# A four-sublayer decoder trunk: two more projections in 512-column form, five state-space tables and twenty modulation rows in other places

## The reference, cut to what matters

```python
cs = silu(c)
for i in range(2):
    mod = cs @ ada_w[i] + ada_b[i]                  # 2048 -> 6 * 2048
    sh1, sc1, g1, sh2, sc2, g2 = split(mod, 6)
    h = rms_norm(x, norm1_g[i]) * (1 + sc1) + sh1
    mix = dilated_attention(h, w_in, w_out) if i == 0 else s5_mixer(h, ...)
    x = x + g1 * mix
    h = rms_norm(x, norm2_g[i]) * (1 + sc2) + sh2
    x = x + g2 * conv_ffn(h, w_up[i], conv_w[i], conv_b[i], w_down[i])   # F = 5632
return rms_norm(x, final_norm_g)
```

## Time and profile before

| what | value |
|---|---|
| time, median of 3 runs | 2733.81 us (2732.66 to 2735.42) |
| time of the profiled execution | 2732.6 us |
| its span (first to last instruction) | 2730.6 us |
| PE busy | 2658.2 us, 97% of the span |
| DVE busy | 2303.9 us, 84% |
| ACT / POOL busy | 1291.1 / 519.4 us |
| HBM traffic | 266 GB/s over the span |

### The profile page before, as it was taken

How to read it: one execution, slowest core, us unless ns; L and a number is a source line. 1 busy time by engine, 2 the same in 40 slices (tenths; PEclk the granted TensorE clock), 3 DMA queues, 4 the chain that set the end, 5 groups by cost and what they waited for, 6 DMA issues and landing times.

```text
span 2730.6 us, 50020 instructions
## 1 busy us (share of the span) xinstructions
PE 2658.2 (97%) x18412; PEld 2375.5 (87%) x18412; DVE 2303.9 (84%) x3390; ACT 1291.1 (47%) x1852; POOL 519.4 (19%) x466
## 2 busy tenths in 40 slices
PE   5999999999999999999999999999999999999998
PEld 2998888888898888888889999999788888888887
DVE  7978988888889999899999989998898975677755
ACT  2444444444434555435555344444365553455542
POOL 4242211101132111000111322244311110011122
PEclk8999999999999999999999999999999999999999
DMA  9989988889876887678888967779777766656663
GB/s 388 385 269 339 347 312 333 318 313 336 312 228 234 297 281 250 204 247 312 280 283 270 376 221 239 235 254 330 258 253 241 257 184 188 196 187 189 182 189 109
DMA packets 241978, 725.45 MB, mean 266 GB/s; under 512 B 51074, under 2 KB 60034, under 8 KB 240898
## 3 DMA queue, kind: packets, MB, share of 16 engines
q1 hardware_dynamic: 185184, 666.98, 71.1%
q10 hardware_dynamic: 56612, 56.01, 6.4%
HBM read 701.66 MB, written 25.44 MB: 266 GB/s over the span
## 4 chain that ended last, share of the span: by engine, by line
PE 83%; DVE 5%; POOL 1%; issue 1%; DMA 1%; ACT 1%; ACTq 0%; POOLq 0%; DVEq 0%
PE proj L1910 39%; PE proj L1913 22%; PE proj L1933 5%; PE proj L1934 4%; PE proj L1935 4%; PE proj L1915 3%; PE proj L1928 1%; DVE w_lo L1181 1%; PE proj L1931 1%; PE ps L2049 1%; PE ps L2139 1%; ACT w_hi L600 1%; DVE ada L1071 0%; DVE work L1115 0%; DVE work L1463 0%
## 5 line engine op out<-in xcount | busy, mean ns | idle before, releaser
L600 ACT ACTIVATE w_hi<-raw 128x1024 fp32r<-128x1024 f32 (+1 forms) x896 | 934.6, 1046 | 999.4 <-PE proj L1913 362.2
L1181 DVE TENSOR_TENSOR w_lo<-raw,w_hi 128x1024 fp32r<-128x1024 f32 (+1 forms) x896 | 1104.8, 1236 | 285.9 <-ACT w_hi L600 275.7
L1910 PE MATMUL proj<-h_hl,w_hi 128*128 128x512 f32 x3990 | 1007.5, 393 | 2.7 <-DVE x L1510 1.8
L1910 PEld LDWEIGHTS proj<-h_hl,w_hi 128*128 128x128 f32 x3990 | 730.5, 189 | 139.3 <-DVE x L1510 2.1
L1913 PEld LDWEIGHTS proj<-h_hl,w_lo 128*128 128x128 f32 x4256 | 580.6, 190 | 41.6
L1913 PE MATMUL proj<-h_hl,w_lo 128*128 128x256 f32 x4256 | 593.4, 282 | 0.0
L1071 DVE SCALAR_TENSOR_TENSOR ada<-ada,held 128x1024 f32<-128x1024 f32 x304 | 396.0, 1303 | 0.0
L1813 POOL TENSOR_TENSOR a_hl<-work,a_hl 128x256 fp32r<-128x256 f32 (+1 forms) x88 | 120.6, 1371 | 1137.3 <-ACT a_hl L880 1137.3
L1933 PE MATMUL proj<-a_hl,w_hi 128*128 128x256 f32 x864 | 245.6, 284 | 0.7 <-DVE a_hl L1401 0.6
L1934 PE MATMUL proj<-a_hl,w_hi 128*128 128x256 f32 x864 | 244.5, 283 | 0.0
L1935 PE MATMUL proj<-a_hl,w_lo 128*128 128x256 f32 x864 | 244.5, 283 | 0.0
(11 more groups left out here) (273 smaller groups left out, 2870.3 us busy)
## 6 DMA issues: line engine op xcount, KB each, us to landing
raw<-in_w_up SPq DMA_DIRECT2D x352, 512.0 KB, 4.9
ada<-in_ada_t SPq DMA_DIRECT2D x304, 512.0 KB, 5.7
raw<-in_w_in SPq DMA_DIRECT2D x224, 512.0 KB, 6.5
raw<-in_w_down SPq DMA_DIRECT2D x128, 448.0 KB, 3.5
raw<-in_w_down SPq DMA_DIRECT2D x64, 512.0 KB, 3.6
ada<-in_ada_w SPq DMA_DIRECT2D x48, 512.0 KB, 8.6
raw<-in_w_out SPq DMA_DIRECT2D x32, 512.0 KB, 5.1
raw<-in_ssm_w_in SPq DMA_DIRECT2D x32, 512.0 KB, 4.9
```

Source lines behind the costliest of these rows:

```text
L600: nc.scalar.activation(w_hi[:, j % LAG, 0:nk * P], raw[:, j % s.ring, 0:nk * P], ACT.Copy).then_inc(hi_ready, 1)
L1181: V.tensor_tensor(w_lo[:, j % LAG, 0:nk * P], raw[:, j % s.ring, 0:nk * P], w_hi[:, j % LAG, 0:nk * P].bitcast(F32), ALU.subtract).then_in ...
L1910: ins = mm(both, w_hi[:, j % LAG, w], hl[:, k].rearrange("p c t -> p (c t)"), start=(k == 0), stop=False)
```

## The change

`attn_out` and `down0b` become wide stages. The 16 tables are no longer all made in `attn_out`: eleven are (steps 3, 5, 7, 10, 12, 15, 17, 20, 22, 25 and 27), and five in `down0b` (steps 16, 21, 26, 31 and 36), in other places of `work` and in `acc`. The 16 modulation rows of `down0b` and four of the eight of `up0b_end` move into `qkv`: its iterations 1 to 5 now have 28 rows in 28 steps. The take of part 19 moves from `down0b` to `up0b_end`. Waits for the last tables' stores move behind `down0b`.

```diff
-WIDE = {"qkv", "up0a", "up0a_end", "down0a", "up0b", "up0b_end", "ssm_out", ...
+TABLES_FIRST = 11
+WIDE = {"qkv", "attn_out", "up0a", "up0a_end", "down0a", "up0b", "up0b_end", "down0b", "ssm_out", ...
@@
-    add("qkv", 6, 14, two, ..., rows=spread(24, 28), begin=spread(20, 20, 8))
+    add("qkv", 6, 14, two, ..., rows=spread(28, 28), begin=spread(20, 20, 8))
@@
-    add("up0b_end", 1, 8, two, rows=spread(8, 16))
-    add("down0b", 1, 16, down, rows=spread(16, 34, 6))
+    add("up0b_end", 1, 8, two, rows=spread(4, 16))
+    add("down0b", 1, 16, down)
@@
+        ef_late, o = cut(work, 2400, 2, 4, 8, 8)
+        tab_a_late, o = cut(work, o, 8, 8, 8)
+        tab_b_late, o = cut(work, o, 8, 8, 8)
+        tab_o_late = [cut(work, o, 8, 64)[0], cut(acc[:, :], 0, 8, 64)[0]]
+        def table_step(n):
+            return 3 + 27 * n // TABLES_FIRST if n < TABLES_FIRST else 16 + 5 * (n - TABLES_FIRST)
@@ ACT
-                    for n in range(KT):
-                        late.setdefault(max(2 * n, 2), []).append(factors(n))
-                        late.setdefault(2 * n + 4 if n > 1 else 4, []).append(store_tab(n))
+                if name in ("attn_out", "down0b"):
+                    for n in range(TABLES_FIRST) if name == "attn_out" else range(TABLES_FIRST, KT):
+                        late.setdefault(max(table_step(n) - 3, 2), []).append(factors(n))
+                        late.setdefault(table_step(n) + 2, []).append(store_tab(n))
@@
-            TAKES = {"up0a_end": (14, 13, 3), "up0b_end": (14, 16, 3), "down0b": (45, 19, 1), ...
+            TAKES = {"up0a_end": (14, 13, 3), "up0b_end": (14, 16, 4), ...
@@ DVE
-                if name == "attn_out":
-                    for n in range(KT):
-                        late.setdefault(2 * n + 2 if n > 1 else 3, []).append(table(n))
+                if name in ("attn_out", "down0b"):
+                    for n in range(TABLES_FIRST) if name == "attn_out" else range(TABLES_FIRST, KT):
+                        late.setdefault(table_step(n), []).append(table(n))
```

More of the change, by code:

```diff
@@ L58 @@
 ADA = 4
-WIDE = {"qkv", "up0a", "up0a_end", "down0a", "up0b", "up0b_end", "ssm_out", "up1a", "up1a_end", "down1a", "up1b",
+TABLES_FIRST = 11
+WIDE = {"qkv", "attn_out", "up0a", "up0a_end", "down0a", "up0b", "up0b_end", "down0b", "ssm_out", "up1a", "up1a_end", "down1a", "up1b",
         "up1b_end", "down1b"}
@@ L139, in plan @@
     add("qkv1", 1, 28, [(PIECE, PIECE, True)], ring=7, old={10 + 2 * k: k for k in range(8)})
-    add("qkv", 6, 14, two, ring=7, old={j: 8 + j for j in range(8)}, rows=spread(24, 28), begin=spread(20, 20, 8))
+    add("qkv", 6, 14, two, ring=7, old={j: 8 + j for j in range(8)}, rows=spread(28, 28), begin=spread(20, 20, 8))
     add("attn_out", 1, 16, two)
@@ L775, in plain, with factors, f, store_tab @@
                 late = {}
+                def factors(n):
+                    def f(i):
+                        act.wait_ge(scores_done, HEADS)
+                        if n >= TABLES_FIRST:
+                            act.wait_ge(gated_ready, FB)
+                        wait(act, tab_made, n - 1)
+                        act.dma_start(table_place(n)[0].rearrange("p a b c -> p (a b c)"), ef_d[n]).then_inc(ef_in_s[n % 2], 16)
+                    return f
+                def store_tab(n):
+                    def f(i):
+                        act.wait_ge(tab_made, n + 1)
+                        act.dma_start(tab_d[n], table_place(n)[3].rearrange("p a b -> p (a b)")).then_inc(tab_out[n % 2], 16)
+                    return f
                 if name == "attn_out":
@@ L911, in _ @@
             for q in range(2):
-                act.wait_ge(tab_out[q], 16 * KT // 2)
+                act.wait_ge(tab_out[q], 16 * ((TABLES_FIRST + 1 - q) // 2))
             def load_tab(n):
@@ L932, in _ @@
                 act.wait_ge(bp_out[q], 16 * KT // 2)
+                act.wait_ge(tab_out[q], 16 * KT // 2)
             act.wait_ge(mod_ready, 20)
@@ L1206, in split_first @@
                 low(st[name])(0, LO_FIRST - 1)
-            TAKES = {"up0a_end": (14, 13, 3), "up0b_end": (14, 16, 3), "down0b": (45, 19, 1), "gate": (33, 20, 1),
+            TAKES = {"up0a_end": (14, 13, 3), "up0b_end": (14, 16, 4), "gate": (33, 20, 1),
                      "ssm_out": (33, 21, 1), "up1a": (41, 22, 1), "up1a_end": (47, 23, 1)}
@@ L1590, in _ @@
                                                                 4: [head1_low]}, keep=True))
-            dve.wait_ge(tab_out[0], 16 * KT // 2)
+            dve.wait_ge(tab_out[0], 16 * ((TABLES_FIRST + 1) // 2))
             norm(1, 0, 3 * KT, 10)
             split_first("ssm_in", ffn(0))
+            dve.wait_ge(tab_out[1], 16 * KT // 2)
             norm(2, 1, 0, 16)
@@ L1851, in _ @@
                 pool.wait_ge(bp_out[q], 16 * KT // 2)
+                pool.wait_ge(tab_out[q], 16 * KT // 2)
             G.memset(c_wide, 0.0).then_inc(cw_clear, 1)
```

25 lines of the change are left out of this document (10 added, 15 removed).

## The result

The changed kernel takes 2738.10 us (median of 20 runs, 2734.79 to 2740.39); the kernel before took 2733.07 in the 20 runs beside it (2731.00 to 2736.92). The ratio is 1.0015, with a 95% interval of 1.0009 to 1.0021: slower by 2.5 to 5.7 us. 2740.0 was forecast, 2735.5 to 2744 as the range.

The account below looks back on a forecast made before the run. PE was taken to set the pace, with DVE nearly full in down0b and attn_out. Terms +9.4 - 0.5 - 0.2 - 3.5 + 0.5 + 0.5 = +6.2 us gave 2738.8 profiled, 2740.0 as median; range 2735.5 to 2744.

Parts of the forecast that it names:

- qkv's heads: qkv loop: new rows at steps 13 and 27 delay POOL's mix, ten heads at 0.94 us each, +9.4 us.
- Rival 1: qkv: POOL's mix ends within its 0.97 us of room, the loop costs nothing, 2730.6 us; chance 0.07.
- Rival 2: qkv: a row locks out one POOL instruction for 1.2 us at most, 0.2 us a head, 2732.9 us; chance 0.06.
- mutual slowing: qkv, beside a head's mix: DVE and POOL slow each other, row 1.76 us instead of 1.2, POOL's last instruction 1.48 instead of 0.61.
- attn_out: attn_out: DVE's 5.67 us per block binds over PE's 5.59; net -0.5 us, and -0.2 at its end.
- the start: Start of attn_out: a table between splits 5 and 6 and two more instructions, mostly covered by PE's piece in hand, 0.8 us.
- down0b: down0b: PE's wide blocks gain 3.5 us, the last tables cost 0.5, the added instruction before the norm +0.5.
- The cushion's terms: down0b: 7.7 us of lead less w_hi 1.05, split 1.22, tail and add 0.9, hand-overs 0.3, written as 4.1 us.
- Rival 3: attn_out and down0b: DVE's backlogs stay within the cushions, PE gains in full, +3.4, 2737.2 us; chance 0.12.
- rival 4: attn_out and down0b: DVE becomes the bound in both, the wide form gives nothing, 2743.5 to 2745 us; chance 0.15.
- The rest: Elsewhere: four rows less in up0b_end, later waits for tab_out and the take of part 19 are free.
- The estimate that the prediction made by the Trainium skill: Wide k-tiles: 327 ns narrow against 325 wide, so 554 k-tiles gain 1.2 us; the rows' 5.9 was used instead.

Follow-up runs that it names:

- experiment 1: Changed kernel with no row at qkv steps 13 and 27 of iterations 1 to 5, two each at steps 3 and 17 instead: 2729.51 us.
- experiment 3: Changed kernel with the rows at qkv steps 13 and 27 of iterations 1 to 5 reading their second operand from PSUM, not SBUF: 2729.36 us.
- Experiment 4: Changed kernel with experiment 1's row places, ten tables in attn_out, later at its start, and six in down0b: 2729.76 us.
- experiment 5: Changed kernel with all modulation rows left where the kernel before has them, 16 of them in down0b: 2745.49 us.
- experiment 2: Kernel before with only the rows moved (20 into qkv, out of up0b_end and down0b), nothing made wide: 2742.68 us.
- Experiment 6: Changed kernel with all 16 tables in attn_out, so down0b is wide with neither rows nor tables: 2745.05 us.

## Why the prediction held, step by step

**qkv's heads, forecast +9.4, measured +8.7.** The step was right: the transposes wait for POOL ten times more, 0.66 us each where 0.7 was said, and the block takes 6.8 instead of 6.9. The head of the earlier trace rows was the right measure; the others have 0.06 us less idle. The second half of the step, that the queue, the bytes and the ten rows of steps 6 and 20 are free, is shown by experiment 1. Rival 1 fell to the ten waits. Rival 2 priced the exclusion at one instruction's length; its mechanism is the right one (experiment 3), its price was not, since POOL's chain holds two instructions there and each was stretched (1.60 and 1.48 against 0.74 and 0.61): 1.73 us, less PE's room of 0.97, is 0.76, against the 0.66 seen. What the prediction called a mutual slowing is this exclusion.

**attn_out, forecast -0.7 with its end, measured -0.4, and the reason given was wrong.** The prediction said that DVE's turn of 5.67 us would bind in every block, with DVE above 95%. It did not: from 813.55 on the block ends are 5.59 apart, PE's own pace, and over the stage DVE is busy for 90%. The step that failed is the price of a table. The prediction took 1.92 us, a table alone, out of a turn of 5.56 in which the table ran beside POOL's squares of x. In the kernel before (the table of 788.54 ends where the next split starts):

```profile
787.57 1.52 POOL L1693 TENSOR_TENSOR square<-x 128x256 f32<-128x256 f32 x1 [8.82 <-DVE x L1510]
789.17 1.07 POOL L1695 TENSOR_TENSOR sumsq<-sumsq,square 128x256 f32<-128x256 f32 x1
791.43 1.22 DVE L1181 TENSOR_TENSOR w_lo<-raw,w_hi 128x1024 fp32r<-128x1024 f32 x1
```

That table took 791.43 - 788.54 = 2.89 us, half as much again as the 1.92 of the one at 779.75, which has no POOL instruction beside it. With 2.89 the same sum gives 5.56 - 2.89 + 0.47 + 0.81 x 2.89 = 5.48 us, under PE's 5.59, and in the kernel after DVE duly has idle time again in the later blocks, first here:

```profile
837.48 1.77 DVE L1201 TENSOR_TENSOR w_lo<-raw,w_hi 128x1024 fp32r<-128x1024 f32 x1 [0.60 <-ACT w_hi L615]
```

What ate the gain was the start, put at 0.8 us: the four block times behind 789.07 are 6.14, 6.18, 6.08 and 6.08, 2.1 us above four of 5.59. There the tables of steps 5, 7, 10 and 12 leave DVE no gap, and a turn with a table in it is 5.56 + 0.47 = 6.03 us. Experiment 4 takes these waits away with the same forms and nearly as many tables, and the stage gains 2.0 us. That the term came out within 0.3 us is luck: a loss in every block was forecast, and one in four blocks was found.

The last head's 0.3 us (its wait is 0.89 here, 0.46 before) came on top and was put at nothing. There, too, POOL's mix lies beside tables and splits of DVE, and its six instructions take 5.45 us in the kernel before, 5.70 in the kernel after and 5.65 in experiment 5, stretched in different places. All experiments have 20.25 to 20.52 us there, experiment 5 with the rows as before and experiment 2 without the wide form among them, so no single edit is its cause; why is left open.

**down0b, forecast -2.5 with its end, measured -2.3.** The blocks come in 7.69 us up to 1579, and then three in 7.87, 8.01 and 7.84: 0.66 us for the last tables, where 0.5 was said. The norm's wait grew by 0.72 (1.13 to 1.85), where the tail's 0.47 was counted. Experiment 6, with no table here, has 124.86 and a wait of 1.65. That the backlog came out so near is in part luck, too: a table took 2.47 to 2.89 us here as well, where 1.92 was counted, and a block without one takes DVE 105.1 / 16 = 6.6 us in experiment 6, where 6.97 was counted, and the two errors offset each other. (The cushion's terms give 4.2, not the 4.1 written.) Rival 3, no stall in either stage, and rival 4, DVE as the bound in both, both fell: each stage stalled in a part of it only.

**The rest, forecast nothing, measured -0.7 in the profiled pair** (-1.6, +0.6, -0.8 and +1.0). These parts have the same work, but the first of them differs by kernel, as said below the table: some -1.7 us that the prediction left out. Of the terms, +8.7 + 0.3 - 0.4 - 2.3 = +6.4 us before rounding stands against the forecast's +6.2; the profiled pair has 5.7, the medians 5.0. So the sum was nearer to the truth than its parts, by an error in `qkv` of -0.7 against +0.3, +0.3 and +0.2 elsewhere.

The estimate that the prediction made by the Trainium skill (TensorE: Matmul & The Clock Gate, section Back-to-back issue gap) is 2.5 ns a k-tile before rounding, 1.4 us for 554 k-tiles and not 1.2. The rows were the better guide: PE's blocks of 16 k-tiles come 5.59 us apart in `attn_out` where 5.76 was the narrow pace, 10 ns a k-tile.

## What to carry to other kernels

An idle gap of an engine is free only if nothing else uses what the gap leaves open: before filling one, look at what runs on POOL in that very gap, and count each instruction of its chain once. When work must move, choose the place within the stage by that, since here two of 28 places held the whole cost of moving 20 rows. The price of an instruction is to be taken where it will run: a table cost DVE 1.92 us alone and 2.89 beside POOL, within one stage, and a sum that mixed the two named the wrong bound. Where a stage's mean load is near that of the bound, its start and end are to be counted apart from its middle.

## What the runs showed of the hardware

The granted clock behind a short idle time of PE is not the same from profile to profile. Ahead of the first matmuls of the stage after `down0a` PE waits 1.74 to 1.76 us in all nine kernels; the eight matmuls behind it then took 2.09 to 2.12 us in seven of them, and 2.73 and 3.21 in the kernel after and experiment 5. The three timelines (before, after, experiment 5):

```profile
1246.25 2.11 PE L1910 MATMUL proj<-h_hl,w_hi 128*128 128x512 f32 x8 [1.75 <-DVE x L1510]
```

```profile
1252.63 2.73 PE L1934 MATMUL proj<-h_hl,w_hi 128*128 128x512 f32 x8 [1.75 <-DVE x L1532]
```

```profile
1243.74 3.21 PE L1934 MATMUL proj<-h_hl,w_hi 128*128 128x512 f32 x8 [1.76 <-DVE x L1532]
```

The windows behind it, of before and of after (the clock is the third number from the end):

```profile
1246.00:1249.00 3.00, 2.75 (x15) 2.41 (x16) 2.83 (x13) 0.00 (x0) 0.00 (x0) 1.00 0.74 254
```

```profile
1252.50:1255.00 2.50, 2.37 (x8) 1.96 (x9) 2.36 (x12) 0.00 (x0) 0.00 (x0) 0.78 0.88 290
1255.00:1258.00 3.00, 3.00 (x14) 2.68 (x14) 2.96 (x8) 1.33 (x2) 0.00 (x0) 0.62 0.82 311
```

The kernel before stays at the higher level (2.4 GHz), the kernel after spends part of its time at the lower (1.2 GHz) and is back at 1.00 from 1258 on. The missing share of clock is 0.22 x 2.5 + 0.38 x 3.0 = 1.7 us of full speed, an estimate of what it costs while PE is the bound. At the norms it is much the same: behind `ssm_out`, after a wait of 2.83 us in both, the root's matmuls start 1972.08 - 1970.03 = 2.05 us after the norm's in the kernel before and 1977.58 - 1974.71 = 2.87 in the kernel after, whose clock is 0.50 from 1975 to 1978. At the norm behind `attn_out` it is the other way round, 2.87 and 2.06 us. So by this estimate a single pair of profiles can differ by a microsecond or two at such a place, and a difference of 5 us has to be read from the medians of 20 runs.
